# Recurrent stage: the bonus and lora products move from the levels into the Gram products, and the next pair's factors are made one level sooner

## What is computed

```python
def rwkv7_step(state, inp):
    r, w, k, v, kk, a = inp
    sa = jnp.einsum('...vk,...k->...v', state, -kk)
    state = (state * w[..., None, :]
             + sa[..., :, None] * (kk * a)[..., None, :]
             + v[..., :, None] * k[..., None, :])
    y = jnp.einsum('...vk,...k->...v', state, r)
    return state, y
...
    w_log = -jax.nn.softplus(-(w0 + jnp.einsum('btdr,drc->btdc', wl, w2))) - 0.5
    a = jax.nn.sigmoid(a0 + jnp.einsum('btdr,drc->btdc', al.reshape(bsz, seq, 2, ICLR_LORA), a2))
    k_dir = k[:, :, None, :] * (1.0 + (a - 1.0) * k_a)
...
    bonus = jnp.sum(rh[:, :, None] * kh * r_k, axis=(2, 4))
    out = (y + bonus[..., None] * vh).reshape(bsz, seq, RWKV_WIDTH)
    return out * g
```

## Time and profile before

| | us |
|---|---|
| median of 3 runs | 1762.81 (1762.13 to 1765.85) |
| the profiled execution, its own time | 1760.1 |
| its span, first to last instruction | 1758.3 |
| of it, from pair 0's first Gram product to pair 3's last tail product | about 190 (156.1 to 346) |
| PE busy, whole span | 1690.9 (96%) |
| mean granted clock of PE | 0.998 |

### The profile page before, as it was taken

One profiled execution on the slowest core, in us unless ns is written; L12 is line 12 of the kernel. 1 busy time (PEld: TensorE's weight loads), 2 busy tenths in 40 slices (PEclk: granted clock), 3 DMA queues, 4 the chain that ended last, 5 costly groups with the idle time before them and its releaser, 6 DMA issues.

```text
span 1758.3 us, 29729 instructions
## 1 busy us (share of the span) xinstructions
PE 1690.9 (96%) x12805; PEld 1381.5 (79%) x12805; DVE 1043.1 (59%) x1308; ACT 815.1 (46%) x1235; POOL 448.2 (25%) x405
## 2 busy tenths in 40 slices
PE   7999888899999999999999999999999999999999
PEld 6877777678888787888877886668887787788877
DVE  5478677356243566766676445975434455675667
ACT  5244545536553433543345236865654343353343
POOL 2002222130100472245310220540010166114620
PEclk9999999999999999999999999999999999999999
DMA  7210000143222565375443222003431275356623
GB/s 253 85 48 2 4 4 28 51 168 120 96 96 72 195 236 180 119 247 185 162 167 107 94 74 72 1 1 120 144 111 43 89 271 189 125 198 233 211 98 140
DMA packets 116926, 212.70 MB, mean 121 GB/s; under 512 B 4248, under 2 KB 50939, under 8 KB 116795
## 3 DMA queue, kind: packets, MB, share of 16 engines
q1 hardware_dynamic: 103239, 159.59, 27.2%
q0 software_dynamic: 13264, 51.09, 8.1%
q10 hardware_dynamic: 291, 0.12, 0.0%
HBM read 185.62 MB, written 25.17 MB: 120 GB/s over the span
## 4 chain that ended last, share of the span: by engine, by line
PE 71%; DVE 11%; ACT 8%; issue 4%; POOL 4%; DMA 3%; DVEq 0%; ACTq 0%; POOLq 0%
PE PS L431 47%; PE PS L538 10%; POOL DW L671 2%; DVE WLO L397 2%; ACT WHI L386 2%; PE PS L1922 1%; DVE SS L2225 1%; DMA diff_dn<-DW 1%; PE PS L1891 1%; PE PS L937 1%; DVE CV L2028 1%; DVE CG L2028 1%; DVE CV L2025 1%; DVE CG L2025 1%; ACT CV L2003 1%
## 5 line engine op out<-in xcount | busy, mean ns | idle before, releaser
L397 DVE TENSOR_TENSOR WLO<-WRAW,WHI 128x2048 fp32r<-128x2048 f32 (+1 forms) x106 | 248.0, 2350 | 296.8 <-ACT WHI L386 296.8
L431 PE MATMUL PS<-HIS,WHI 128*128 128x512 f32 x856 | 335.0, 391 | 5.0 <-DVE CV L2028 1.8
L431 PE MATMUL PS<-HIS,WLO 128*128 128x512 f32 x856 | 333.2, 389 | 0.0
L431 PE MATMUL PS<-LOS,WHI 128*128 128x512 f32 x856 | 333.1, 389 | 0.0
L386 ACT ACTIVATE WHI<-WRAW 128x2048 fp32r<-128x2048 f32 (+1 forms) x107 | 203.2, 1907 | 230.3 <-PE PS L431 182.9
L431 PE MATMUL PS<-WHI,HIS 128*128 128x512 f32 x608 | 240.1, 395 | 0.2 <-DVE LOS L728 0.2
L431 PE MATMUL PS<-WLO,HIS 128*128 128x512 f32 x608 | 237.0, 390 | 0.0
L431 PE MATMUL PS<-WHI,LOS 128*128 128x512 f32 x608 | 236.6, 389 | 0.0
L431 PEld LDWEIGHTS PS<-HIS,WHI 128*128 128x128 f32 x856 | 160.6, 188 | 42.4 <-DVE CV L2028 4.0
L431 PEld LDWEIGHTS PS<-HIS,WLO 128*128 128x128 f32 x856 | 160.7, 188 | 33.7
L431 PEld LDWEIGHTS PS<-LOS,WHI 128*128 128x128 f32 x856 | 160.7, 188 | 33.2 <-issue 0.2
(11 more groups left out here) (331 smaller groups left out, 2838.5 us busy)
## 6 DMA issues: line engine op xcount, KB each, us to landing
WRAW<-ffn_w_up SPq DMA_DIRECT2D x88, 512.0 KB, 5.0
RW<-ffn_w_down POOLq DMA_DIRECT2D x22, 1024.0 KB, 7.4
diff_dn<-DW POOLq DMA_DIRECT2D x22, 1024.0 KB, 5.3
WRAW<-cross_wkv SPq DMA_DIRECT2D x16, 1024.0 KB, 5.0
PW<-diff_dn SPq DMA_DIRECT2D x8, 1536.0 KB, 9.1
WRAW<-diff_w_in SPq DMA_DIRECT2D x12, 1024.0 KB, 5.2
...
```

The lines of the kernel that those rows point to most:

```text
L397: V.e.tensor_tensor(part(WLO[place(i)], i), part(WRAW[raw_slot[i]], i), part(WHI[place(i)], i).bitcast(F32), ALU.subtract).then_inc(S("w_l ...
L431: mm = e.matmul(o, l, r, start=(si == 0 and kk == 0 and q == 0), stop=(si == len(steps) - 1 and kk == nk - 1 and q == 2))
```

## The change

- The bonus product and both lora products leave the sides and stand in `gram_pe`, in banks 2 and 3: lora 0 of the next pair behind A, bonus ahead of KAP 0, lora 1 ahead of KAP 1. ACT's answers (two `prep_tanh_act` and the copy to BON) stand at the head of `pair_act`, ahead of level 0.
- The sides now are: s = 2 transposes of BET, s = 4 of KAP, s = 6 of AR, s = 8 the value products as before; s = 3, 5 and 7 are empty on PE. For pair 3, s = 3 and 5 hold the gates.
- DVE makes the next pair's factors in levels 1 to 4 (scan, key, scale, and the split-off `prep_bonus_dve`), ACT its exponentials at s = 5, the end of level 2. For pair 0 the four `sgu_low_dve` move from level 1 to levels 0 and 2, two each.
- Waits follow: the Gram products wait behind A for `p_qfree` (ACT's copy of the pair before out of bank 2), bonus for ACT's first tanh (`p_lorafree`), lora 1 for the copy to BON (`p_bonfree`).

```diff
@@ gram_pe
         mm.then_inc(S("p_a"), 1)
+        if j > 0:
+            e.wait_ge(S("p_qfree"), j)
+        if j + 1 < NJ:
+            lora_pe(e, j + 1, 0, 2)
 
         for l, d, b in ((BET, 0, 6), (BET, 1, 0), (KAP, 0, 4), (KAP, 1, 6)):
+            if (l, d) == (KAP, 0):
+                bonus_pe(e, j)
+            elif (l, d) == (KAP, 1) and j + 1 < NJ:
+                e.wait_ge(S("p_bonfree"), j + 1)
+                lora_pe(e, j + 1, 1, 2)
@@ new
+    def bonus_pe(e, j):
+        e.wait_ge(S("p_bonus"), j + 1)
+        if j + 1 < NJ:
+            e.wait_ge(S("p_lorafree"), 2 * j + 3)
+        for d in range(2):
+            mm = e.matmul(PS[:, 2, :], rk("bones"), TMP[1][:, d, :], start=(d == 0), stop=(d == 1))
+        mm.then_inc(S("p_bonmm"), 1)
@@ side_pe
-        if s == 2:
...
-                mm = e.matmul(PS[:, 6, :], rk("bones"), TMP[1][:, d, :], start=(d == 0), stop=(d == 1))
...
-                lora_pe(e, j + 1, 0, 6)
...
-                lora_pe(e, j + 1, 1, 6)
...
+        if s in (3, 5) and j + 1 == NJ:
+            e.wait_ge(S("p_tokfree"), 3 * j + s // 2)
+            gates_pe(e, s - 3)
+        elif s in (2, 4):
...
+                    mm = e.transpose(PS[:, 6 + d, t * P:t * P + P], (BET, KAP)[s // 2 - 1][:, d, t * P:t * P + P], ident)
+            mm.then_inc(S("p_tok"), 1)
+        elif s == 6:
+            e.wait_ge(S("p_tokfree"), 3 * j + 2)
@@ side_act
+        elif s == 5:
+            prep_exp_act(e, j + 1)
@@ pair_act
+        if j + 1 < NJ:
+            prep_tanh_act(e, j + 1, 0, 2)
+        e.wait_ge(S("p_bonmm"), j + 1)
+        e.activation(BON[j][:, :], PS[:, 2, :], ACT.Copy).then_inc(S("p_bonfree"), 1)
+        if j + 1 < NJ:
+            prep_tanh_act(e, j + 1, 1, 2)
@@ pair_dve
-            elif j == 0 and lv == 1:
-                for g in range(SGU_G):
-                    sgu_low_dve(e, g)
+            if j == 0 and lv in (0, 2):
+                sgu_low_dve(e, lv)
+                sgu_low_dve(e, lv + 1)
...
-            if j + 1 < NJ and lv >= 2:
-                (prep_scan_dve, prep_key_dve, prep_scale_dve)[lv - 2](V, j + 1)
+            if j + 1 < NJ and lv >= 1:
+                (prep_scan_dve, prep_key_dve, prep_scale_dve, prep_bonus_dve)[lv - 1](V, j + 1)
```

84 lines of the change are left out of this document (32 added, 52 removed).

## The result

The changed kernel takes 1765.41 us, median of 12 runs (1763.46 to 1769.48), against 1762.1 for the kernel before (1760.7 to 1766.21). The ratio is 1.0017, with a 95% interval from 1.0009 to 1.0025: about 3 us slower. A second measurement gave 1.0024 [1.0011, 1.0037]. The forecast was 1762.0 us, 0.85 less than the 1762.81 measured by then for the kernel before, and no measurable change. The time lies inside the forecast's range, but the change went the other way, by more than its measurement is uncertain.

What follows compares the result with a forecast made beforehand. PE, busy for 96% of the span, was taken as the bound. Pairs 1, 2, 3 and 0 summed as -0.5 + 0.4 - 0.8 + 0.05 = -0.85 us: 1759.25 profiled, 1762.0 median, range 1757.0 to 1767.3.

Steps and rivals of the forecast that it cites:

- part 1: Levels to Gram parts: moved products cost PE the same in both, 4.1 us a pair, 1.7 in pair 3; worth nothing.
- The clock: Whole kernel: PE's granted clock was read as full throughout; no term for a lower clock.
- The Gram parts (parts 1 and 2): Gram parts, pairs 0 to 3: moved work arrives in full; waits net of shape changes +0.2, -0.45, -0.45, -0.1 us.
- Part 3, the term for DVE in pair 0: Levels of pair 0: +0.6 us for DVE, within a levels sum of -0.15.
- a level sooner, free nothing: Next pair's factors made one level earlier: no gain, since no Gram part had waited for them.
- Rival 3: Levels 1 and 2, pairs 0 to 2: POOL's BET product delays DVE's scan, 2.2 us a pair; 1767.6, chance 0.23.
- Both of its signs: Level 2: PE waits for DVE's XX or QT, and L1591's successor takes well above 1.43 us.
- Pairs 1 and 2 in the levels: Levels 1 to 4: pair 1 changes by -0.05 us, pair 2 by +0.85; about 22.4 and 22.9 us long.
- Pair 3 in the levels: Levels 1 to 4: waits ahead of AR transposes and level 4 go, a block's end costs +0.45; 25.0 us long.
- A rule of the notes against the rows: PE's instruction blocks of 256: rows show at least 3.46 us each, with stops; the skill calls crossing mostly hidden.

Runs made afterwards that it cites:

- the second execution: Profiled execution of the unaltered changed kernel, measured again: span 1762.0 us; that measurement's median 1766.25 us, 1.0024 of the kernel before.
- the factors back: Changed kernel with its second half undone (DVE, ACT factors and low parts at their old levels), PE's new order kept: 1762.94 us, 1.0003 of the kernel before.
- in pieces: Output projection's 1 MB weight loads split in four and spread: kernel before 1757.11 us, again 1759.67; change 1764.56; with the factors back 1760.54.
- the first execution: Profiled execution of the changed kernel in its first measurement: 1769.48 us, the slowest of its runs (median 1765.41).
- the 64 fillers: 64 waiting instructions among the first GEMMs: added to the kernel before, 1767.55 us (1.0031); to the change with the factors back, 1769.88 us (1.0036).

## Why the prediction was wrong

The sum had two halves, PE's own time and its waits. Added up over the stage, the forecast had +1.0 us for the first (0.25 for shapes in each Gram part) and -1.85 for the second. Measured in the stage are +4.3 and -1.2 in the second execution, +6.8 and -1.9 in the first. The half on which the prediction spent its care came out; the half that it called worth nothing did not.

- **The step that failed: part 1, "it leaves the levels and comes back in the Gram part, in full".** It came to the Gram parts as forecast (PE's busy time there grew by 14.8 us, 15.0 counted). It did not leave the levels in full: 11.6 us at full clock, where 14.0 were counted (4.1 in each of pairs 0 to 2, 1.7 in pair 3). The products themselves had cost 0.26 us a pair less in the levels than counted, and what else stands there became 1.6 us longer. So TensorE's new order by itself makes PE's own time 3.1 us longer, and 1.0 was counted. With the factors back shorter waits make up for this (idle time 24.8 us before, 21.0 then), and the kernel stands at 1.0003.
- **The clock was put at nothing**, without a reason beyond the full clock of the one execution at hand. In pair 0's levels 3.4 us at 1.2 GHz cost 1.4 to 1.5 us in either execution of the change; the execution of the kernel before has no such stretch in its stage, but of its two executions in pieces one has. Over whole runs the two kernels have the same mean clock, so this explains the profiled executions better than it explains the medians.
- **The Gram parts (parts 1 and 2) were right.** Forecast 10.3, 10.8, 9.6 and 9.5 us, measured 10.42, 11.06, 9.47 and 8.77. The wait ahead of pair 0's bonus was put at 1.5 us and is 1.39. The stop in KAP of pair 1 and most of that in BET of pair 2 are gone, as forecast. Only pair 3 came out 0.7 shorter, because its stop was not there to stay: it had been a fetch behind a load.
- **Part 3, the term for DVE in pair 0, was too small, without being the loss.** It stood as +0.6, with no working; the trace has 2.4 us of waits for X. The forecast counted the scan a level sooner but did not ask what POOL would have beside it: the scale takes 0.68 us in pair 0 of the kernel before, with POOL idle, and already 1.43 in its pair 1, beside a POOL instruction of 1.05. But the waits for ACT in the same levels fell from 4.3 us to 1.5 and 2.2, and the sum of both was forecast at 4.1 and is 4.0 and 4.6. That the sum is right with both terms off is luck.
- **The factors "a level sooner, free nothing"** was right as far as it goes, and hid a price. Back in their old place they save 0.0014 to 0.0021 of the time, and 0.0023 with the loads in pieces: 2.5 to 4 us. In the traces it is a number of small differences in waits and stops, 2.5 us over the stage. Which of them the time hangs on is open.
- **Rival 3 had a mechanism that is there, at a price that is not.** POOL's BET product does hold up DVE's work ahead of the scan, as its rows said, and the Trainium skill's lock between the two engines (SBUF — State Buffer, Who interferes with whom) agrees: the scale takes 0.68 us alone, 2.78 beside the product in pair 0, 1.92 and 1.90 in pairs 1 and 2. It was priced at 2.2 us in each of pairs 0 to 2. PE waited 1.6 us for it in pair 0, where other waits became shorter in turn, and 0.5 and 0.4 us for the chain sums in pairs 1 and 2. Taken away alone it gives 1.0009, which the intervals do not tell from the change. Both of its signs came, a wait for XX in level 2 and the scale well above 1.43 us, and still they are not the loss. I gave this rival 0.23; that 1765.4 lies between its 1767.6 and the forecast does not bear it out.
- **Pairs 1 and 2 in the levels.** Pair 1 was right in sum (22.18 for 22.4; the second execution 21.91). Pair 2 missed by 0.9 and 0.6 us; the block's end in level 3's X products, of which 0.15 was counted, stopped PE for 0.91 and 0.62, and that makes most of it. The one in the value products came as forecast (0.42 for 0.5).
- **Pair 3 in the levels failed outright**: 25.0 us forecast, 29.40 and 27.88 measured, for 27.36 before. The forecast counted +0.45 for a block that ends in the value products and got 2.24 and 2.00; behind it the first execution has 6.8 us at 1.2 GHz, the second none, which may be why they differ by 1.5. With the loads in pieces these levels take 25.70 us. The trace of before held the warning in the earlier trace rows: 4.99 us for a block, at 208 GB/s of other transfers. I read this as a slower fetch and did not ask whose transfer it was, nor when the changed order would meet the next.
- **The tails**, not counted, changed by -0.3 us in all. That is luck: pairs 0 to 2 became 2.0 to 2.9 us longer, and pair 3 2.4 to 3.2 shorter, because its stops had met a load before. In pieces, where they no longer do, the tails are 2.7 to 3.0 us longer with the change.
- **A rule of the notes against the rows.** The forecast had weighed the Trainium skill's statement that the crossing of a 256-instruction block is mostly hidden (Runtime: NRT & Kernel Launch, Instruction fetch mechanics) and kept to the rows. The runs bear the rows out: stops that the profile calls issue take 14.5 us of the stage before and 14.2 and 13.2 after, and 64 instructions that cost next to nothing where they stand made two kernels 5.5 to 6 us longer, the clock's part included.

What stays open: why PE's products take longer at the places that the new order gives them; on which of the small waits the early factors' price hangs; and what the 64 fillers cost behind the stage, beside the lower clock.
